# Expert weights in a streamed mixture of experts: gate and up pieces handled in halves

## The reference, cut to what matters

```python
def run_chunk(args):
    xc, e = args
    return (jax.nn.silu(xc @ w_gate[e]) * (xc @ w_up[e])) @ w_down[e]
```

## Time and profile before

| | us |
|---|---|
| median of 3 runs | 1628.4 |
| lowest and highest | 1627.89 and 1629.53 |
| the profiled execution | 1626.63 |
| its span, first to last instruction | 1624.9 |

### The profile page before, as it was taken

How to read it: one execution, slowest core, us unless ns; L and a number is a source line. 1 busy time by engine, 2 the same in 40 slices (tenths; PEclk the granted TensorE clock), 3 DMA queues, 4 the chain that set the end, 5 groups by cost and what they waited for, 6 DMA issues and landing times. The chain is left out here.

```text
span 1624.9 us, 19653 instructions
## 1 busy us (share of the span) xinstructions
PE 1562.9 (96%) x7484; PEld 728.3 (45%) x7484; DVE 715.9 (44%) x1551; ACT 309.4 (19%) x646; POOL 41.0 (3%) x58
## 2 busy tenths in 40 slices
PE   8999999999999999979999999999999999999996
PEld 4444463444444444345654444555344444444442
DVE  2222246343433333357265489824534343434335
ACT  2000122000000000022234277823100000000002
POOL 0000000000000000000000000000000000000000
PEclk9999999999999999999899999999999999999999
DMA  6262509999999999955210300063999999999993
GB/s 207 78 243 93 189 36 394 419 420 419 420 419 420 420 420 420 420 207 165 78 52 26 144 13 1 1 252 129 402 419 420 419 420 421 419 421 420 419 419 155
DMA packets 111644, 457.52 MB, mean 282 GB/s; under 512 B 29359, under 2 KB 55983, under 8 KB 62384
## 3 DMA queue, kind: packets, MB, share of 16 engines
q1 hardware_dynamic: 106352, 448.23, 68.8%
q0 software_dynamic: 5184, 7.88, 1.3%
HBM read 460.78 MB, written 6.29 MB: 287 GB/s over the span
## 5 line engine op out<-in xcount | busy, mean ns | idle before, releaser
L1040 PE MATMUL ps<-raw,e_xT 128*64 128x512 f32 x2112 | 467.9, 593 | 17.9 <-DMA raw<-in_expert_w_up 17.1
L1040 PEld LDWEIGHTS ps<-raw,e_xT 128*64 128x64 f32 x2112 | 153.0, 137 | 318.0 <-issue 315.8
L1193 DVE TENSOR_TENSOR e_sg_hid<-e_sg_hid,ps 64x512 f32<-64x512 f32 x66 | 44.9, 681 | 400.9 <-ACT e_sg_hid L1118 400.9
L1067 PE MATMUL ps<-raw,e_hT 128*64 128x512 f32 x880 | 203.4, 600 | 3.9 <-DVE e_hT L1201 1.0
L1173 DVE TENSOR_TENSOR x_res<-x_res,ps 128x512 f32<-128x512 f32 x268 | 171.1, 682 | 3.3 <-PE ps L1077 1.2
L441 PE MATMUL ps<-c_hT,raw 128*128 128x512 f32 x384 | 165.2, 592 | 0.9 <-DMA raw<-in_conv_w_in 0.9
L1126 ACT ACTIVATE e_yhi<-ps,e_wtab 128x512 fp32r<-128x512 f32 x66 | 45.4, 688 | 422.0 <-PE ps L1067 397.9
L1889 PE MATMUL ps<-a_spare,raw 128*128 128x512 f32 x256 | 117.2, 615 | 4.5 <-DVE a_spare L1650 4.5
L1118 ACT ACTIVATE e_sg_hid<-ps 64x512 f32<-64x512 f32 x66 | 39.2, 593 | 420.6 <-PE ps L1040 420.6
L1077 PE MATMUL ps<-e_yhi,e_pick 64*128 64x512 f32 x528 | 111.7, 418 | 3.5 <-DVE x_res L1173 2.6
L441 PEld LDWEIGHTS ps<-c_hT,raw 128*128 128x128 f32 x384 | 72.8, 190 | 92.0 <-issue 90.9
(11 more groups left out here) (302 smaller groups left out, 1349.2 us busy)
## 6 DMA issues: line engine op xcount, KB each, us to landing
raw<-in_expert_w_gate SPq DMA_DIRECT2D x128, 1024.0 KB, 25.9
raw<-in_expert_w_up SPq DMA_DIRECT2D x128, 1024.0 KB, 27.0
raw<-in_expert_w_down SPq DMA_DIRECT2D x108, 1024.0 KB, 26.1
e_raw<-in_expert_w_down SPq DMA_DIRECT2D x20, 1024.0 KB, 26.2
raw<-in_conv_w_in SPq DMA_DIRECT2D x11, 1024.0 KB, 10.0
raw<-in_w_kv SPq DMA_DIRECT2D x6, 1024.0 KB, 6.9
raw<-in_conv_w_out SPq DMA_DIRECT2D x1, 4096.0 KB, 18.9
raw<-in_attn_w_in SPq DMA_DIRECT2D x4, 1024.0 KB, 5.3
```

What stands on the lines that cost most here:

```text
L1040: mm = pe.matmul(ps_gu[C - C * i:2 * C - C * i, :], xT[:, q % 2, k, u * C:(u + 1) * C], ring(m, L, p)[:, kk * F:(kk + 1) * F], start=(k == ...
L1067: mm = pe.matmul(ps_y[n * C:(n + 1) * C, :], hT[:, 2 * h + kk, :], ring(m, L, p)[:, kk * D + n * 512:kk * D + (n + 1) * 512], start=(h == ...
```

## The change

A gate or up piece is moved as two transfers of 512 KB, each with two of its four feature groups and a semaphore of its own: a partition's part is then a run of 4 KB. Down pieces stay whole. `load_half` takes the place of `load_piece`; `parts(p)` is 2 for gate and up and 1 for down. SP asks for the halves in the order gate 0, up 0, gate 1, up 1 of a round, then for the next round, then for the two down pieces, and waits before each for the same half of the piece that lay there. PE waits before the first product of each half, for gate and up apart, and `s_used` rises at the last product of each half: ten times for a chunk (NUSE), so all counts of `s_used` are rewritten.

```diff
-def load_piece(sp, m, L, p, e):
+def load_half(sp, m, L, p, j, e):
...
-    sp.dma_start(ring(m, L, p), w).then_inc(m.load[L][p % NR], 16)
+    part = slice(j * PIECE // parts(p), (j + 1) * PIECE // parts(p))
+    sp.dma_start(ring(m, L, p)[:, part], w[:, part]).then_inc(m.load[L][p % NR, j], 16)
...
+def half_number(p, j):
+
+    e, i = p // NPIECE, p % NPIECE
+    return NUSE * e + (4 * (i // 2) + 2 * j + i % 2 if i < 4 else 4 + i)
...
-        def freed(p):
-
-            return p + 1 if p < NPIECE * TWICE else p + 1 + NPIECE
+        def freed(p, j):
+
+            return half_number(p, j) + 1 + (0 if p < NPIECE * TWICE else NUSE)
...
-                for p in pieces:
-                    wait(pe, load[p % NR], p // NR * 16 + 16)
                 for kk in range(4):
                     k = 4 * b + kk
                     for i, p in enumerate(pieces):
+                        if kk % 2 == 0:
+                            wait_half(pe, p, kk // 2)
...
-                        if kk == 3:
+                        if kk % 2:
                             mm.then_inc(s_used, 1)
...
-            wait(act, s_used, c * NPIECE + 4)
+            wait(act, s_used, c * NUSE + 8)
...
-                for p in range(NPIECE * place, NPIECE * (place + 1)):
+                for p, j in ((NPIECE * place + i, j) for first in (0, 2, 4) for i, j in
+                             (((first, 0), (first + 1, 0), (first, 1), (first + 1, 1)) if first < 4 else
+                              ((4, 0), (5, 0)))):
                     if p >= NR:
-                        sp.wait_ge(s_used, freed(p - NR))
-                        load_piece(sp, m, L, p, e)
+                        sp.wait_ge(s_used, freed(p - NR, j))
+                        load_half(sp, m, L, p, j, e)
```

More of the change, by code:

```diff
@@ L50 @@
 PIECE = 2048
+NUSE = 10
 NR0 = 16
@@ L157, in load_semaphores, with parts @@
 def load_semaphores(m, L):
-    m.load[L] = [m.sem(f"load{L}_{q}") for q in range(NR)]
+    m.load[L] = {(q, j): m.sem(f"load{L}_{q}_{j}") for q in range(NR) for j in range(parts(q))}
+def parts(p):
+    return 2 if p % NPIECE < 4 else 1
 def moe_memory(nc, m, L, ctx):
@@ L472, in load_piece @@
     w = w[e] if isinstance(e, int) else w[bass.ds(e, 1)].rearrange("e p n -> (e p) n")
-    sp.dma_start(ring(m, L, p), w).then_inc(m.load[L][p % NR], 16)
+    part = slice(j * PIECE // parts(p), (j + 1) * PIECE // parts(p))
+    sp.dma_start(ring(m, L, p)[:, part], w[:, part]).then_inc(m.load[L][p % NR, j], 16)
 def prefetch(sp, m, L, pieces):
     for p in pieces:
-        load_piece(sp, m, L, p, p // NPIECE)
+        for j in range(parts(p)):
+            load_half(sp, m, L, p, j, p // NPIECE)
+def half_number(p, j):
+    e, i = p // NPIECE, p % NPIECE
+    return NUSE * e + (4 * (i // 2) + 2 * j + i % 2 if i < 4 else 4 + i)
 def by_k(x):
@@ L973, in first_piece, with wait_half @@
             return NPIECE * (c if c <= TWICE else c - 1)
-        def freed(p):
-            return p + 1 if p < NPIECE * TWICE else p + 1 + NPIECE
+        def freed(p, j):
+            return half_number(p, j) + 1 + (0 if p < NPIECE * TWICE else NUSE)
+        def wait_half(pe, p, j):
+            pe.wait_ge(load[p % NR, j], p // NR * 16 + 16)
         def y_place(c):
@@ L1063, in pe_down @@
                 p = first_piece(c) + 4 + h
-                wait(pe, load[p % NR], p // NR * 16 + 16)
+                wait_half(pe, p, 0)
                 for kk in range(2):
@@ L1114, in act_step @@
         def act_step(act, c):
-            wait(act, s_used, c * NPIECE + 4)
+            wait(act, s_used, c * NUSE + 8)
             wait(act, s_hid, c)
             act.activation(sg, ps_gu[C:2 * C, :], ACT.Silu).then_inc(s_sg, 1)
-            wait(act, s_used, c * NPIECE + 6)
+            wait(act, s_used, c * NUSE + 10)
             if c == 0:
@@ L1145, in dve_turned @@
             dve.wait_ge(s_xt, n - 1)
-            wait(dve, s_used, (2 * q - 4) * NPIECE + 2 * NPIECE)
+            wait(dve, s_used, (2 * q - 2) * NUSE)
             dve.tensor_tensor(xT[:, q % 2, h * HK:(h + 1) * HK, :], turn_bank(n)[:].rearrange("p (k s) -> p k s", k=HK),
@@ L1199, in dve_step @@
             wait(dve, s_ht, c + 1)
-            wait(dve, s_used, c * NPIECE)
+            wait(dve, s_used, c * NUSE)
             dve.tensor_copy(hT[:].rearrange("p k c -> p (k c)"), ps_h[:, 0:KF * C]).then_inc(s_hev, 1)
@@ L1260, in end @@
                 for n in range(2):
-                    sp.wait_ge(s_used, freed(last_piece(c, (n,))))
+                    sp.wait_ge(s_used, freed(last_piece(c, (n,)), 0) + (parts(last_piece(c, (n,))) - 1) * 2)
                     feature_weights(sp, m, n)
```

## The result

The changed kernel takes 1640.2 us (median of 4 runs, 1638.63 to 1641.49), the kernel before beside it 1628.1 us (1625.29 to 1629.53). The ratio is 1.0077 with a 95% interval of 1.0065 to 1.0090: slower by 12.1 us. The profiled execution has a span of 1636.9 us where before had 1624.9.

What follows compares the result with a forecast made beforehand. The prediction took the weight stream through the DMA engines, not PE, as the bound. Pace +21.1 us, work behind the last landing -4.3 and start 0 gave +16.8, on 1628.4 1645.2 us; range 1634 to 1656.

Steps and rivals of the forecast that it cites:

- What bounds the kernel: Experts of both layers: the weight stream at 420 GB/s, 14.98 us a set against PE's 13.61 us a chunk.
- Part 1: Pace of the experts' weight stream: +0.091 us a gate or up piece, +21.1 us in both layers.
- the two quiet stretches: 107 to 115, convolution's output weights in 4 KB runs, 409 GB/s; 117 to 121, expert pieces in 8 KB runs, 422.
- The row at 421 GB/s: 923 to 928: attention's output weights in 4 KB runs, no slower than 8 KB; the prediction took 409 instead.
- Part 2: Start of the stream in a layer: first refill about 1.7 us sooner, priced at 0.
- Part 3: PE's work behind the last up landing: 3 products instead of 8, -2.2 us a layer, -4.3 us in both.
- Part 4: Costs nothing: more waits on PE, ten SP issues a set instead of six, more prefetch issues, new counts for ACT and DVE.
- Runs of 4 KB are free: Rival: the experts' stream stays at 420 GB/s, leaving only -4.3 us, 1624.1 us; chance 0.07.
- A third of the price: Rival: a gate or up piece costs 0.02 to 0.035 us more, 1628.7 to 1632.2 us; chance 0.12.
- SP or the queue: Rival: a queue of fixed transfer number holds 6 MB instead of 10, or SP issues too slowly; 1660 to 1700 us, chance 0.04.
- the signs announced: Experts: 411 to 413 GB/s, about 148,500 packets, refill 1.7 us sooner, last round broken, up transfer on chain 15 to 20 us.
- PE waits more in total by some 15 us: Sign for PE in the experts: more frequent, shorter waits, with a total some 15 us larger.

Runs made afterwards that it cites:

- e2: The kernel before, gate and up pieces still one transfer each, but in runs of 4 KB or 2 KB: 1649.8 us (ratio 1.0144) and 1677.3 us (1.0318).
- e3: The changed kernel, but PE waits for both halves of gate and up before a round's first product: 1642.8 us, ratio 1.0098.
- e8: The kernel before, with gate and up of sets 8 to 30 as 2 MB transfers (16 KB runs), set 31 in halves: 1624.2 us, ratio 0.9979.
- e11: The kernel before, with 2 MB gate and up transfers for sets 8 to 26, 8 KB runs for 27 to 30, set 31 halved: 1619.7 us, ratio 0.9956.
- e4: The changed kernel, but SP frees and refills whole pieces instead of halves: 1642.5 us, ratio 1.0088.
- e5: The changed kernel, but only the last set's gate and up are split in halves, all others whole with 8 KB runs: 1624.2 us, ratio 0.9979.
- e1: The kernel before, but each gate or up piece moved as two transfers of 64 partitions with 8 KB runs: 2417 us.

## Why the prediction was right, and where its sum was off

The prediction said 1645.2 us and slower with 0.84; measured 1640.2, within the range. By its own steps:

- **What bounds the kernel: the stream of weights.** Held. A slower stream alone moved the layers' ends later (e2), and PE's larger waits in the middle had no say (e3). In the other direction the stream became faster (e8) but the ends followed only when no transfer of 2 MB stood near them (e11), and there PE's own pace meets the stream's.
- **Part 1, the pace: the mechanism right, the term too large.** It said +0.091 us a piece, +21.1 us; measured 8.85 / 114 = 0.078 and 8.00 / 114 = 0.070 us a piece, +16.9 us in both layers. This is the step where most of the miss of 5.0 us sits, 4.2 us of it. Its part for the runs, 0.079 from the two quiet stretches, was nearly right (0.074). Its part for the second transfer's completions, 0.012 a piece or 2.8 us in both layers, was not: after and the 4 KB run of e2 have the same rate within 0.2 GB/s with twice and once the transfers, so that it is 0.002 at most. I had taken the whole gap between 420 and 422 GB/s as a bound and then as the price. The row at 421 GB/s (4 KB runs at a granted clock of 0.50) was rightly passed over.
- **Part 2, the start: 0, and so it came (11.39 to 11.36, 12.34 to 12.29), but not for the reason given.** The prediction held that the queue still had work at the first refill, so that an earlier issue was worth nothing. In before the first refilled gate piece lands 5.2 us after its issue in layer 0 and 6.2 in layer 1, where the shortest of all is 5.0: the queue was all but empty. Why the earlier issue gave nothing even so isn't shown. e4 hints that it is worth about 1 us a layer; the halves themselves would then have cost as much in the same place.
- **Part 3, behind the last landing: right in kind, a fifth too large.** -2.2 us a layer forecast, -1.8 measured; e3 takes it away and the 3.79 us are back. Five products fewer were priced at 0.43 us each; the rows have 3.65 - 1.93 = 1.72 us for them. The 0.43 was the wrong unit: a gate and an up product run together in 0.86, and one alone takes 0.86 too. Other rows say the same: fourteen records behind a wait take 3.65 us as sixteen do (e5), thirty take 7.08 where thirty-two take 7.04 (e8). Behind the last up half the up product runs beside the gate product of the next group, and the last up product alone. That is two such steps instead of four, and 2 x 0.86 = 1.72. The prediction announced 1.4 us of records there; 1.93 stand.
- **Part 4, free: held.** The packets rose as counted, a gate or up issue takes 0.33 to 0.43 us where there is room, and there is no sign of SP being late: a DMA share of 1.02 over both long stretches. What it said of PE's waits, that one which is already met costs next to nothing, holds for such waits. One that isn't met and parts a gate product from its up product costs more: the 80 extra starts above. Here they lay beside the stream.
- **What is left.** Parts 1 and 3 as measured give 16.85 - 3.64 = +13.2 where +16.8 was forecast, 3.6 less. The -1.2 us outside the experts and the base (1628.1 instead of 1628.4) make up 1.5 more: 5.1, the whole miss to the rounding.
- **The rivals.** "Runs of 4 KB are free" fell with the 412 GB/s, in four kernels. "A third of the price" fell as well: it needed 0.035 us a piece at most. "SP or the queue" half happened. The view of the tile raw on SP has the issues and landings in after as follows (ns least, median, most; then us from issue to landing):

```profile
L480 SPq DMA_DIRECT2D raw<-in_expert_w_gate x256: 327/468/3312, 100.5 to 1587.8; - x128
L480 SPq DMA_DIRECT2D raw<-in_expert_w_up x256: 328/1032/5726, 104.0 to 1589.0; - x128
...
DMA to landing us min/median/max: 4.9/17.3/21.6
```

The landings come after 17.3 us in the median where 25.6 stood, so the queue does hold less work than before. The rival's reason, a fixed number of transfers, fits these two kernels alone. In e2 the transfers are as large and as many as in before, and the same line of the view reads, with 4 KB and then with 2 KB runs:

```profile
DMA to landing us min/median/max: 5.0/19.4/24.2
DMA to landing us min/median/max: 4.9/15.0/20.2
```

From 400 to 620 some 10 transfers were on their way in before, 11 in after, 7 in e2 at 4 KB and 5 at 2 KB, with SP held in its issues in all four (an up issue takes 1.0 to 2.3 us in the median). So the number isn't fixed: more runs in a transfer leave fewer of them on the way. In none did a gap open in the full stream, and the price of it was nothing.

Of the signs announced, four came (412 GB/s, 148,514 packets, refill sooner by 1.7 us, the chain through an up transfer of 18.6 us). "PE waits more in total by some 15 us" is true by 13.7 us, but only if busy and idle time are read together; by PE's idle time alone it looks false. The refill is in these rows of SP in after, where 1150.00 - 1148.03 (the layer's first product) = 1.97 us stand for 3.7:

```profile
1145.95 0.33 SPq L480 DMA_DIRECT2D e_raw<-in_expert_w_down  x1
1150.00 0.33 SPq L480 DMA_DIRECT2D raw<-in_expert_w_gate  x1
1150.37 0.43 SPq L480 DMA_DIRECT2D raw<-in_expert_w_up  x1
```

## What to carry to other kernels

Where a stream of weights is the bound, price a change of its shape by the number of runs for each DMA engine (here about 9 ns a run, at 16, 8, 4 and 2 KB), not by the number of transfers. Fine pieces pay only where someone waits for the last of them, and a wait that parts two products which would run together makes PE look busy with half the work. Split the last set, keep the runs long before it, and see that the coarsest transfers end early enough that nobody near the end waits for a whole one. And before filling a wait with work from behind it, ask what that work was hiding.

## What the runs showed of the hardware that I had not expected

- Two transfers to 64 adjacent partitions each, one after the other, run at about 189 GB/s with every DMA engine shown busy, against 420 for transfers to 128 partitions with the same runs of 8 KB (e1).
- Two transfers of 512 KB instead of one of 1 MB cost nothing measurable in a full queue: 412.2 and 412.3 GB/s (after against e2 at 4 KB).
- What is on its way in a full queue is bounded neither by a number of transfers nor by their bytes: some 10 transfers of 1 MB with runs of 8 KB (before), 7 and 5 with two thirds of the bytes in runs of 4 and 2 KB (e2), 11 where two thirds are in transfers of 512 KB (after).
- A gate and an up product of 64 columns each run together, 0.86 us for both, and one that has to go without its partner takes as long: 160 lone records and 80 starts more in after, 25.8 us more of busy time for the same 2,112 records.
